# Turning the expert activations of the first table: 32x32 blocks on VectorE and transfers between partition quarters, in the place of TensorE transposes

## The reference

```
q    = x @ w_q                         # 8 heads x 2 halves of 128
top 16 of 128 keys in each half, top 16 of their 256 sums -> eid[t, h, k], g = softmax
a    = <x[t], u_tab[eid]>              # u_tab: 16384 experts x 2048
coef = g * gelu(a)
y[t] = sum over h, k of coef * v_tab[eid]
```

## Time and profile before

| | us |
|---|---|
| median of three runs | 3892.0 |
| lowest and highest | 3887.9, 3896.21 |
| span of the profiled execution | 3886.0 |
| TensorE busy in it | 3860.9 |
| VectorE busy in it | 2538.5 |
| ScalarE busy in it | 2066.4 |

### The profile page before, as it was taken

One profiled execution on the slowest core, in us unless ns is written; L12 is line 12 of the kernel. 1 busy time (PEld: TensorE's weight loads), 2 busy tenths in 40 slices (PEclk: granted clock), 3 DMA queues, 4 the chain that ended last, 5 costly groups with the idle time before them and its releaser, 6 DMA issues.

```text
span 3886.0 us, 60298 instructions
## 1 busy us (share of the span) xinstructions
PE 3860.9 (99%) x19852; PEld 3290.0 (85%) x19852; DVE 2538.5 (65%) x3843; ACT 2066.4 (53%) x3240; POOL 168.7 (4%) x148
## 2 busy tenths in 40 slices
PE   9999999999999999999999999999999999999999
PEld 8989988888888888888899889888888888888887
DVE  5565788878886555555565555888788875555555
ACT  5354444478885444444454544444688874444444
POOL 2110000010000000000121000000100000000000
PEclk9999999999999999999999999999999999999999
DMA  5445555555445555555454555555555455555655
GB/s 197 148 167 177 185 184 184 185 173 172 168 170 184 195 198 196 196 197 196 162 178 147 168 176 187 185 187 184 179 169 171 169 173 196 196 198 202 201 196 182
DMA packets 194890, 707.08 MB, mean 182 GB/s; under 512 B 22256, under 2 KB 22448, under 8 KB 194400
## 3 DMA queue, kind: packets, MB, share of 16 engines
q1 hardware_dynamic: 190800, 692.21, 52.8%
q0 software_dynamic: 3984, 13.37, 0.9%
HBM read 699.20 MB, written 6.29 MB: 182 GB/s over the span
## 4 chain that ended last, share of the span: by engine, by line
PE 97%; DVE 1%; DMA 1%; ACT 1%; issue 0%; DVEq 0%; SPq 0%; ACTq 0%
PE ps L2099 12%; PE ps L2101 12%; PE ps L2100 12%; PE ps L2023 12%; PE ps L2025 12%; PE ps L2024 12%; PE ps L1689 4%; PE ps L1690 4%; PE ps L1691 4%; PE ps L2076 2%; PE ps L2037 1%; PE ps L1772 1%; PE ps L1774 1%; PE ps L1773 1%; PE ps L1984 1%; PE ps L1982 1%
## 5 line engine op out<-in xcount | busy, mean ns | idle before, releaser
L1087 DVE TENSOR_TENSOR w_lo<-w_raw,w_hi 128x1024 fp32r<-128x1024 f32 x1312 | 1636.2, 1249 | 1225.8 <-ACT w_hi L588 1211.9
L588 ACT ACTIVATE w_hi<-w_raw 128x1024 fp32r<-128x1024 f32 x1312 | 1389.9, 1061 | 1592.6 <-DMA w_raw<-in_v_tab 757.4
L2023 PE MATMUL ps<-w_hi,act_lo_t 128*128 128x512 f32 x2048 | 807.9, 394 | 0.5 <-ACT stage L967 0.3
L2025 PE MATMUL ps<-w_hi,act_hi_t 128*128 128x512 f32 x2048 | 800.5, 391 | 0.0
L2099 PE MATMUL ps<-w_hi,act_lo_t 128*128 128x512 f32 x2048 | 797.1, 389 | 0.0
L2101 PE MATMUL ps<-w_hi,act_hi_t 128*128 128x512 f32 x2048 | 796.8, 389 | 0.0
L2024 PE MATMUL ps<-w_lo,act_hi_t 128*128 128x512 f32 x2048 | 796.7, 389 | 0.0
L2100 PE MATMUL ps<-w_lo,act_hi_t 128*128 128x512 f32 x2048 | 796.7, 389 | 0.0
L2025 PEld LDWEIGHTS ps<-w_hi,act_hi_t 128*128 128x128 f32 x2048 | 384.2, 188 | 85.3
L2101 PEld LDWEIGHTS ps<-w_hi,act_hi_t 128*128 128x128 f32 x2048 | 384.4, 188 | 80.2
L2099 PEld LDWEIGHTS ps<-w_hi,act_lo_t 128*128 128x128 f32 x2048 | 384.5, 188 | 79.7 <-DVE act_lo_t L1593 0.2
(11 more groups left out here) (249 smaller groups left out, 2908.0 us busy)
## 6 DMA issues: line engine op xcount, KB each, us to landing
w_raw<-in_u SPq DMA_DIRECT2D x512, 512.0 KB, 3.4
w_raw<-in_v_tab SPq DMA_DIRECT2D x512, 512.0 KB, 3.5
w_raw<-in_dense SPq DMA_DIRECT2D x288, 512.0 KB, 3.5
x_spill<-big POOLq DMA_DIRECT2D x16, 256.0 KB, 4.5
big<-x_spill POOLq DMA_DIRECT2D x32, 128.0 KB, 3.9
big<-in_x_in SPq DMA_DIRECT2D x4, 512.0 KB, 5.4
big<-in_keys POOLq DMA_DIRECT2D x2, 1024.0 KB, 7.1
out<-big SPq DMA_DIRECT2D x8, 256.0 KB, 2.2
```

Of the source, the lines that this page charges most:

```text
L588: act.activation(w_hi[:, slot, :], w_raw[:, slot, :], ACT.Copy).then_inc(s_hi, 1)
L1087: dve.tensor_tensor(w_lo[:, slot, :], w_raw[:, slot, :], w_hi[:, slot, :].bitcast(F32), ALU.subtract).then_inc(s_lo, 1)
L2023: pe.matmul(o, act_lo_t[:, kb, t], w_hi[:, s % 4, c], start=kb == 0, stop=False)
L2025: ins = pe.matmul(o, act_hi_t[:, kb, t], w_hi[:, s % 4, c], start=False, stop=kb == KB - 1)
```

## The change

Turns 0 to 13 (`SHUFFLED` = 14) of each layer are turned in another way; turns 14 to 31 keep the TensorE transposes.

- TensorE: `upright` is left out for turns 0 to 13.
- ScalarE: gelu writes `stage` in another order of columns (expert quarter and expert block exchanged), and waits for VectorE (`s_mix`), not for TensorE (`s_upright`), before it overwrites `stage`. Gelu of `tb` 1 thus waits for VectorE's turning of `tb` 0.
- VectorE: in the place of `mix` a `turn_quads` transposes the 32x32 blocks of `stage` into `turned_t` (two buffers, at columns 15360 to 17407 of `big`). The loop over items is unrolled by two, and two turns stand before it. The loop over the scattering turns is unrolled fully.
- SyncE's queue: 16 transfers a turn, `shuffle`, move 32 partitions each from `turned_t` to `big`, four behind each of the loads of slabs 3, 4, 5 and 6, two turns later (turn j's with the loads of turn j+2). Each waits for `s_mix`.
- `big` has another layout inside a turn's 1024 columns: (token quarter, token block, expert block, 32 tokens) instead of (expert block, 256 tokens). `mix`, `spread`, `c_hi`, `c_lo` and the first block's halves read and write it through patterns with runs of 32 (4 in `spread`).
- GpSimd fills the columns of `turned_t` with ones in a second instruction, after all the shuffles; VectorE waits for all the shuffles before the first `one_hots` of turn 15, and for both fills in turn 16.

```diff
+                def shuffle(j, b, a):
+                    sp.wait_ge(s_mix, j * 2 + (2 * U_TURNS * layer + 2))
+                    for q in range(QUADS):
+                        dst = big[32 * q:32 * (q + 1), bass.ds(j * 1024 + 256 * a, 256)]
+                        sp.dma_start(dst.rearrange("p (b x) -> p b x", b=TB),
+                                     turned_t[32 * a:32 * (a + 1), b, :, P * q:P * (q + 1)]).then_inc(s_shuffled[b], 16)
...
+                with sp.Fori(0, SHUFFLED // 2) as j:
+                    for b in range(2):
+                        for s in range(8):
+                            u_load(j * 2 + (2 + b), s)
+                            if 3 <= s < 7:
+                                shuffle(j * 2 + b, b, s - 3)
...
-                pool.memset(at(DIRECT * T, (N_KEYS - DIRECT) * T), 1.0).then_inc(s_ones, 1)
+                pool.memset(at(K_TURNED + 2048, N_KEYS * T - K_TURNED - 2048), 1.0).then_inc(s_ones, 1)
+                for b in range(2):
+                    pool.wait_ge(s_shuffled[b], 256 * (SHUFFLED // 2 * (layer + 1)))
+                pool.memset(at(K_TURNED, 2048), 1.0).then_inc(s_ones, 1)
...
-                    if not (isinstance(m, int) and m == 0):
-                        act.wait_ge(s_upright, m)
-                    act.activation(stage[:, :], bank(u_bank(i, tb)), ACT.Gelu).then_inc(s_gelu, 1)
+                    if shuffled or (isinstance(i, int) and i == SHUFFLED and tb == 0):
+                        if not (isinstance(m, int) and m == 0):
+                            act.wait_ge(s_mix, m)
+                    else:
+                        act.wait_ge(s_upright, lin(i, 2, (2 * U_TURNS - 2 * SHUFFLED) * layer + tb - 2 * SHUFFLED))
+                    if shuffled:
+                        act.activation(stage[:, :].rearrange("p (a q e) -> p q a e", a=QUADS, q=4),
+                                       bank(u_bank(i, tb)).rearrange("p (q a e) -> p q a e", a=QUADS, q=4),
+                                       ACT.Gelu).then_inc(s_gelu, 1)
...
+                def turn_quads(i, tb, b):
+                    dve.wait_ge(s_gelu, i * 2 + (2 * U_TURNS * layer + tb + 1))
+                    if tb == 0 and not (isinstance(i, int) and i < 2 and layer == 0):
+                        dve.wait_ge(s_shuffled[b], i * 128 + (256 * (SHUFFLED // 2 * layer) - 128 * b))
+                    dve.transpose(turned_t[:, b, tb, :], stage[:, :]).then_inc(s_mix, 1)
...
                         if turn is not None and s in (4, 6):
-                            mix(turn, s // 2 - 2, None)
+                            turn_quads(turn, s // 2 - 2, b)
...
+                    grid = at(0, N_KEYS * T).rearrange("p (c a b q f) -> p b a c q f", a=QUADS, b=TB, q=4, f=32)
+                    dst = grid[:, t0 // P, t0 % P // 32, :, :, t0 % 32:t0 % 32 + 4]
+                    dve.tensor_tensor(dst, dst, whole_w[:, :, :].rearrange("p (c q) k -> p c q k", q=4),
+                                      ALU.mult).then_inc(s_g, 1)
...
+                for b in range(2):
+                    dve.wait_ge(s_shuffled[b], 256 * (SHUFFLED // 2 * (layer + 1)))
                 one_hots(0, 0)
...
-                        if s in (1, 3) and not (isinstance(i, int) and i == 0):
+                        if s in (1, 3) and (scattering or isinstance(i, int) and i > SHUFFLED):
                             upright(before(i), s // 2)
```

More of the change, by code:

```diff
@@ L261, in decoder_kernel @@
         s_upright = S("s_upright")
+        s_shuffled = [S(f"s_shuffled{b}") for b in range(2)]
         s_mix = S("s_mix")
@@ L343, in turned, with whole_turn, expert_block @@
             return ps[:, b:b + 2, o:o + P]
+        turned_t = at(K_TURNED, 2048).rearrange("p (i b e) -> p i b e", i=2, b=TB)
+        def whole_turn(turn):
+            a = big[:, 1024 * turn:1024 * (turn + 1)] if isinstance(turn, int) else big[:, bass.ds(turn * 1024, 1024)]
+            return a.rearrange("p (a b q f) -> p q b a f", a=QUADS, b=TB, q=4)
+        def expert_block(i, q):
+            return whole_turn(i * 2 + q // 4)[:, q % 4]
         def xs(tb, c):
@@ L395, in _, with u_load @@
                 n0 = SLAB0["u", layer]
[L396 to L398 removed]
+                def u_load(i, s):
+                    load(s % RING, i * 8 + (n0 + s), u[bass.ds(i * 8 + s, 1)].rearrange("a p n -> (a p) n"))
+                def shuffle(j, b, a):
[4 more added lines that the diff above has]
+                                     turned_t[32 * a:32 * (a + 1), b, :, P * q:P * (q + 1)]).then_inc(s_shuffled[b], 16)
+                with sp.Fori(0, 2) as i:
+                    for s in range(8):
+                        u_load(i, s)
+                with sp.Fori(0, SHUFFLED // 2) as j:
+                    for b in range(2):
+                        for s in range(8):
+                            u_load(j * 2 + (2 + b), s)
+                            if 3 <= s < 7:
+                                shuffle(j * 2 + b, b, s - 3)
+                with sp.Fori(SC_FIRST, U_TURNS) as i:
+                    for s in range(8):
+                        u_load(i, s)
                 n0 = SLAB0["vt", layer]
@@ L994, in u_turn @@
                             weighted(i, s)
+                        shuffled = not scattering and not (isinstance(i, int) and i > SHUFFLED)
                         if s == 1:
-                            gelu(before(i), 0)
+                            gelu(before(i), 0, shuffled)
                         if s == 4 and not (isinstance(i, int) and i == 0):
-                            gelu(before(i), 1)
+                            gelu(before(i), 1, shuffled)
                 act.wait_ge(s_spill, 16 * PIECES * (layer + 1))
@@ L1473, in mix @@
                     m = 2 * U_TURNS * layer + tb
[L1474 to L1479, removed]
+                    dve.wait_ge(s_upright, i * 2 + (m + 1) - 2 * SHUFFLED * (layer + 1))
+                    rows = whole_turn(i)[:, :, tb]
+                    new = bank(UPRIGHT).rearrange("p (q a f) -> p q a f", q=4, a=QUADS)
                     if isinstance(i, int) and i < SC_FIRST - 1 or spreads is None:
@@ L1511, in experts @@
                 dve.wait_ge(s_spill, 16 * PIECES * (layer + 1))
-                with dve.Fori(0, ITEMS - 2) as i:
-                    topk_turn(i + 2, i * 8 + (ubase + 8), range(8), i)
+                for b in range(2):
+                    topk_turn(2 + b, ubase + 8 * (1 + b), range(8), b, b)
+                with dve.Fori(1, SHUFFLED // 2) as i:
+                    for b in range(2):
+                        topk_turn(i * 2 + (2 + b), i * 16 + (ubase + 8 * (1 + b)), range(8), i * 2 + b, b)
                 chain(dve.tensor_copy(csum[:, :], cv[:, :, 0:1].rearrange("p i k -> p (i k)")))
@@ L1582, in experts, with quads, c_lo, first_lo @@
                 scatter_turn(0)
-                with dve.Fori(1, SC_TURNS - 1) as i:
+                for i in range(1, SC_TURNS):
                     scatter_turn(i)
-                scatter_turn(SC_TURNS - 1)
                 vbase = SLAB0["vt", layer]
                 m0 = N_KEYS * layer
[L1590 to L1596, removed]
+                def quads(x):
+                    return x.rearrange("p (b a f) -> p b a f", b=TB, a=QUADS)
+                def c_lo(i, q, buf):
+                    dve.wait_ge(s_chi, i * V_TURN + (m0 + q + 1))
+                    dve.tensor_tensor(quads(act_lo_t[:, buf, :]), expert_block(i, q),
+                                      quads(act_hi_t[:, buf, :].bitcast(F32)), ALU.subtract).then_inc(s_clo, 1)
+                def first_lo(tb):
+                    return dve.tensor_tensor(quads(act_lo_t[:, 0, :])[:, tb], expert_block(0, 0)[:, tb],
+                                             quads(act_hi_t[:, 0, :].bitcast(F32))[:, tb], ALU.subtract)
                 last = SC_TURNS * 4
```

43 lines of the change are left out of this document (24 added, 19 removed).

## The result

The changed kernel takes 3931.46 us (median of 4 runs, 3931.18 to 3932.87); the kernel before, on the same chip, 3892.38 us (3887.9 to 3896.21). The ratio is 1.0103, with a 95% interval from 1.0090 to 1.0116: 39 us slower. I had said 3882 us, 10 us faster, with a range up to 3904. The direction was wrong and the time lies outside the range.

A forecast was written before the change was run, and what follows sets the result against it. TensorE was taken to bound the kernel, VectorE's loop close beside it. Turn 22.40 - 0.10 + 0.10 = 22.40 against 22.77, 0.37 x 28 = 10 us won: 3892 - 10 = 3882 us, range 3866 to 3904.

The forecast's parts named there:

- The ceiling of 26 us: TensorE: 56 sets of transposes removed at 0.47 us each, 26 us or 0.96 a turn, the most to be won.
- The loop through VectorE, turn 22.40 + c: Load 3, rounding, lo 3 to lo 6 make TensorE wait at slab 6; about 0.6 of 0.96 us lost.
- c = -0.1: VectorE: two transposes at 0.69 us replace two copies of 0.69, with 0.1 us less for address work before them.
- Rivals 1 and 2: VectorE transposes: 1, 0.41 us each, turn 21.84, 3866 us, chance 0.13; 2, 1.22 each, turn 23.46, 3911 us, chance 0.12.
- The transfers, 0.1 us a turn: DMA traffic of the 448 shuffles: 1.1% by bytes, 0.1 us a turn added for late landings such as load 3's.
- SyncE's queue, "It fits, barely ... Cost zero": Four shuffles behind each of loads 3 to 6 take 1.7 to 2.4 us, plus the load's own, against 2.72 a slab.
- the 0.9 us: SyncE's queue: loads 4 to 7 and the next slab 0 can come late by some 0.9 before lo feels it.
- Rival 3: SyncE's queue or transfers become the limit, from 0.58 us an issue; at 0.9 us an issue 3907 us, chance 0.10.
- The seam: VectorE's wait for all shuffles before turn 15's one-hots, and the split fill of ones: zero cost.

The follow-up runs named there:

- experiment 5: Changed kernel without transfers, with VectorE's top-k steps reordered to 4, 4, 4, 1, 3, 1, 5, 3 behind the eight lo: 3868.11 us, ratio 0.9938.
- experiment 2: Changed kernel without the 448 transfers and the waits for them, VectorE still turning the quads: 3884.37 us, ratio 0.9973.
- experiment 3: Changed kernel with the same 16 transfers a turn on SyncE's queue, two behind each of eight loads: 3892.75 us, ratio 0.9998.
- experiment 1: Changed kernel with TensorE transposing again in turns 0 to 13 and no transfers, new layout and unrolling kept: 3893.50 us, ratio 0.9999.
- experiment 4: Changed kernel with the 448 transfers issued by GpSimd as soon as both token blocks are turned: 3903.40 us, ratio 1.0025.
- experiment 11: Changed kernel with transfers issued by GpSimd in one burst and VectorE's top-k steps evened out: 3873.48 us, ratio 0.9952.

## Why the prediction was wrong, point by point

*The ceiling of 26 us* is right: 26.0 by the windows of experiment 5.

*The loop through VectorE, turn 22.40 + c* is right. The turn without transfers is 22.45, and the gain 9 us of 26. The forecast for that case, without my 0.1 for the transfers, was 22.30, 13 us of gain, so the 9 is met less well than the mechanism. In turn 10 of experiment 2 the way to lo 3 takes 5.03 where I had 4.81, since the load takes 3.50 and lo 3 begins 0.12 after its rounding; the run to the end of lo 6 takes 11.74 where I had 11.89. With the run from lo 3 to lo 6 shortened the other 16 come back. *c = -0.1* was -0.25 in that turn: the transposes take 0.711 us each (I took 0.69), the hops before them fell from 0.26 and 0.24 to 0.14 and 0.13, and the lo behind them are a little shorter. Rivals 1 and 2 are both off. The lower bound of 0.41 for a transpose, on which rival 1 stood, doesn't follow from the earlier trace rows: 512 floats at that row's rate take 0.57, and the copies from PSUM take 0.69, so it isn't twice their pace. With 0.57 rival 1's turn would have been 22.16, not 21.84.

*The transfers, 0.1 us a turn*, was too low: 0.28 in experiment 3, 8 us in all. The share by bytes, 1.1%, said nothing of what the transfers do to a load that lands at the same time. The page after shows the queue's packets:

```profile
q1 hardware_dynamic: 226640, 706.92, 55.7%
```

Against the earlier trace rows a shuffle's 80 packets hold each of the 16 engines 0.31 us, where bytes alone give 0.10 and packets alone 0.86: three times the share that I had taken.

*SyncE's queue, "It fits, barely ... Cost zero"* is the step that failed. Its term was 1.7 to 2.4 us for four shuffles; measured 2.94 from the first to the end of the fourth, and 3.72 from load to load. I had priced a shuffle by the earlier trace rows, both with one end in HBM and in rows of 4096 and 512 bytes, and the earlier trace rows was misread: it is a single issue of `gain`, not a load behind a load. The trace of before held none of the shuffle's form. A term that fits a gap of 2.72 by 0.0 to 0.7 us, with its own price from another kind of instruction, was not a zero. Nor could the 0.9 us cover it: four slabs late by 1.0 make 4.0. The cost is the difference of the changed kernel to experiment 3, 38.7 us. Added up, the runs give 9 us won without transfers, 8 lost by landings, 39 by the bunches: 38 lost, 39 measured (by the windows 8.9, 8.0 and 40.3, 39.3 lost).

*Rival 3* had the mechanism and the right point, 0.58 us an issue, with a chance of 0.10, and its time was wrong as well: 3907 at 0.9 us an issue, where 0.629 (0.77 with the gap between) gave 3931. Two things were missing in it: that the turn can't be shorter than the queue's steps in a line (the sum of 23.9 above, 23.5 where load 3 leaves with slab 0), however much slabs 7 to 2 give back, and the backlog of loads that leave together and land late.

The Trainium skill (DMA: Bandwidth & Descriptors, section Rules for kernel authors) says that small transfers pay mostly overhead and should be merged. I set it aside because two loads can be under way at once. That is so: the landing of a shuffle overlaps others. Its 0.629 us on the queue doesn't, and 16 of it a turn is what was paid for here. Whether merging them would help is not shown; no run has fewer and larger transfers.

*The seam* is small but not zero: VectorE waits for the last shuffles 2.5 us in 2 times, turn 15 is 0.6 us longer in each layer, and turn 16 of layer 0 0.8, together 2.0. Some 3 us more of the 45.2 between the two profiled executions lie between the start of the last turn of layer 0 and that of the first of layer 1, a stretch that varies by as much among the other runs (1246.3 us before, 1249.5 after, 1247.4 in experiment 1, 1251.8 in experiment 2).

Two things stay open: whether both ends in SBUF or the short rows make a transfer hold the queue longer, and the 0.14 us between two shuffles, which was not taken apart (one register instruction of 0.046 us per shuffle is a part of it).

## What to carry to other kernels

Before small transfers are put on a queue that also issues just-in-time loads, count the queue as an engine: the load's slot, plus the issue and the gap of each small transfer, against the time between two loads, by a row of the same kind of transfer; if there is none, take the time as unknown on the dear side. The same transfers spread evenly cost 8 us where four behind one load cost 47. And before the busiest engine is relieved, find the loop that runs beside it with little slack (here 0.3 us of 22.7, at an engine that is 86% busy) and reorder its work first: the two changes together won 22 us, each alone nothing.

## What the runs showed of the hardware

- The time that a DMA holds its issuing queue goes with the form of the transfer, not with its bytes: 0.333 us for a load of 512 KB from HBM, 0.509 to 0.629 for 16 and 32 KB from SBUF to SBUF on SyncE's queue. GpSimd's line shows 0.54 for the same shuffle that takes 0.629 on SyncE:

```profile
L593 POOL DMA_DIRECT2D big<-big x448: 533/542/634, 471.5 to 2743.7; - x150
```

- Small transfers delay a large load on DMA engines that are busy 0.63 to 0.70 of the time (0.57 without them): in the middle of the turns, 512 KB land 0.1 to 0.4 us later with two shuffles a slab, and load 3 0.7 (experiment 4) and 1.4 us (experiment 11) later with a burst of 16.
- A 32x32-block transpose of 128x512 floats on VectorE takes 0.711 us, close to a copy of that size out of PSUM (0.69).
